# The latent attention's up-projections in three passes of split operands

## The reference

```python
def _mla(c_q, c_kv, k_r, z, cq_g, ckv_g, w_uq, w_ukv, q_g, k_g, cos, sin):
    bn, s, _ = c_q.shape
    q = (_rmsnorm(c_q, cq_g) @ w_uq).reshape(bn, s, MLA_HEADS, MLA_QK)
    kv = (_rmsnorm(c_kv, ckv_g) @ w_ukv).reshape(bn, s, MLA_HEADS, MLA_NOPE + MLA_V)
    k_nope, v = kv[..., :MLA_NOPE], kv[..., MLA_NOPE:]
    ...
    q = _rmsnorm(q, q_g)
    k = _rmsnorm(k, k_g)
```

## Time and profile before

| | |
|---|---|
| median of 3 runs | 1043.36 us (1043.26 to 1048.55) |
| span of the profiled execution | 1042.3 us |
| PE busy | 1016.2 us (97%) |
| DVE busy | 747.5 us (72%) |
| ACT busy | 571.0 us (55%) |
| DMA | 160.57 MB, mean 154 GB/s |
| chain that ended last | PE 86%, DVE 6%, ACT 3%, issue 3%, DMA 2% |

### The profile page before, as it was taken

How to read it: one execution, slowest core, us unless ns; L and a number is a source line. 1 busy time by engine, 2 the same in 40 slices (tenths; PEclk the granted TensorE clock), 3 DMA queues, 4 the chain that set the end, 5 groups by cost and what they waited for, 6 DMA issues and landing times.

```text
span 1042.3 us, 21750 instructions
## 1 busy us (share of the span) xinstructions
PE 1016.2 (97%) x9147; PEld 933.6 (90%) x9147; DVE 747.5 (72%) x1188; ACT 571.0 (55%) x841; POOL 71.9 (7%) x177
## 2 busy tenths in 40 slices
PE   9999999999999999999999999789999999999997
PEld 8878999999977999999998898769899899998885
DVE  5879677778777966778789868746778566555445
ACT  5775576444666658444468575125345466565333
POOL 8600000020000000001140000000000000000000
PEclk9999999999999999999999999999999999999999
DMA  9645453485664545348777350001355356555552
GB/s 320 187 135 164 141 152 113 153 259 167 190 184 134 150 136 160 115 145 243 171 194 215 109 166 24 24 22 43 122 168 180 123 160 182 177 186 183 193 189 81
DMA packets 73553, 160.57 MB, mean 154 GB/s; under 512 B 6917, under 2 KB 16320, under 8 KB 73456
## 3 DMA queue, kind: packets, MB, share of 16 engines
q1 hardware_dynamic: 70304, 150.59, 45.7%
q0 software_dynamic: 2832, 8.06, 4.0%
q10 hardware_dynamic: 320, 0.53, 0.1%
HBM read 158.11 MB, written 1.05 MB: 153 GB/s over the span
## 4 chain that ended last, share of the span: by engine, by line
PE 86%; DVE 6%; ACT 3%; issue 3%; DMA 2%; ACTq 0%; POOL 0%; DVEq 0%; POOLq 0%
PE psum L470 23%; PE psum L472 23%; PE psum L471 22%; PE psum L881 2%; PE psum L1033 1%; PE psum L870 1%; DVE ring_lo L1387 1%; DMA ring<-in_w_branch 1%; PE psum L722 1%; PE psum L700 1%; DVE arena L1573 1%; PE psum L1307 1%; PE psum L714 1%; PE psum L1324 1%; PE psum L704 1%
## 5 line engine op out<-in xcount | busy, mean ns | idle before, releaser
L1387 DVE TENSOR_TENSOR ring_lo<-ring,ring_hi 128x1024 fp32r<-128x1024 f32 (+4 forms) x291 | 342.4, 1194 | 175.2 <-ACT ring_hi L2446 173.3
L2446 ACT ACTIVATE ring_hi<-ring 128x1024 fp32r<-128x1024 f32 (+4 forms) x291 | 297.7, 1034 | 267.9 <-PE psum L472 241.9
L470 PE MATMUL psum<-hT,ring_hi 128*128 128x256 f32 x904 | 257.8, 285 | 2.5 <-issue 1.5
L472 PE MATMUL psum<-hT,ring_lo 128*128 128x256 f32 x904 | 255.0, 282 | 0.0
L471 PE MATMUL psum<-hT,ring_hi 128*128 128x256 f32 x904 | 254.7, 282 | 0.0
L470 PEld LDWEIGHTS psum<-hT,ring_hi 128*128 128x128 f32 x904 | 171.7, 190 | 5.1 <-issue 4.5
L472 PEld LDWEIGHTS psum<-hT,ring_lo 128*128 128x128 f32 x904 | 171.8, 190 | 0.0
L471 PEld LDWEIGHTS psum<-hT,ring_hi 128*128 128x128 f32 x904 | 171.7, 190 | 0.0
L470 PE MATMUL psum<-ring_hi,hT 128*128 128x512 f32 (+4 forms) x416 | 156.1, 375 | 2.1 <-DVE ring_lo L1387 1.5
L472 PE MATMUL psum<-ring_hi,hT 128*128 128x512 f32 (+4 forms) x416 | 151.9, 365 | 0.0
L471 PE MATMUL psum<-ring_lo,hT 128*128 128x512 f32 (+4 forms) x416 | 151.6, 364 | 0.0
(11 more groups left out here) (461 smaller groups left out, 1355.1 us busy)
## 6 DMA issues: line engine op xcount, KB each, us to landing
ring<-in_w_in SPq DMA_DIRECT2D x104, 512.0 KB, 3.4
ring<-in_w_ff SPq DMA_DIRECT2D x64, 512.0 KB, 3.5
ring<-in_w_branch SPq DMA_DIRECT2D x24, 512.0 KB, 3.5
ring<-in_w_out SPq DMA_DIRECT2D x24, 512.0 KB, 3.6
ring<-in_w_in SPq DMA_DIRECT2D x24, 384.0 KB, 3.3
ring<-in_w_xkv SPq DMA_DIRECT2D x16, 512.0 KB, 3.6
ring<-in_w_in SPq DMA_DIRECT2D x8, 528.0 KB, 3.6
ring<-in_w_xq SPq DMA_DIRECT2D x8, 512.0 KB, 3.8
```

What stands on the lines that cost most here:

```text
L470: mm(b, lhs[0], rhs[0], start=start, stop=False, **how)
L472: return mm(b, lhs[1], rhs[0], start=False, stop=stop, **how)
L1387: V.tensor_tensor(chunk_view(ring_lo, RAW, c), chunk_view(ring, RAW, c), plain(chunk_view(ring_hi, RING_HI, c)), ALU.subtract).then_inc(ev ...
L2446: AC(chunk_view(ring_hi, RING_HI, c), chunk_view(ring, RAW, c), ACT.Copy).then_inc(ev("whi_ready"), 1)
```

## The change

The up-projections use `split_mm`. For that the high halves of `wuq` and `wukv` are copied by ACT behind slot 1's copies, as soon as the layer's small weights have landed; DVE makes high and low halves of `cT` behind its copies, and the low halves of the two weights around the low half of chunk 15. PE waits for DVE's halves (`clo_ready`, `ulo_ready`) in place of the copies of `cT` and the landed weights. The low halves of the weights take the place of the weights themselves, the high ones lie in the arena where the gates come later.

```diff
+        cT_hi, cT_lo = at(arena_r, 3584, 3, S), at(arena_r, 4352, 3, S)
+        wuq_hi, wuq_lo = at(arena_r, 1024, 2, MH * MQK), at(arena_r, PB + 2048, 2, MH * MQK)
+        wukv_hi, wukv_lo = at(arena_r, 2560, 1024), at(arena_r, PB + 3584, 1024)
...
-                copied(pe, ("cT", l, 0), ("cT", l, 1))
-                pe.wait_ge(ev("layer_in"), 16 * N_LAYER_DMA * (l + 1))
+                pe.wait_ge(ev("clo_ready"), l + 1)
+                pe.wait_ge(ev("ulo_ready"), 2 * (l + 1))
                 for t in range(T):
+                    rows_t = slice(t * P, (t + 1) * P)
                     for h in range(2):
                         b = open_bank(pe, ("uq", l, t, h))
                         for k in range(2):
-                            m = mm(b[:, 0:384], cT[:, k, t * P:(t + 1) * P], wuq[:, k, h * 384:(h + 1) * 384],
-                                   start=(k == 0), stop=(k == 1))
+                            m = split_mm(b[:, 0:384], (cT_hi[:, k, rows_t], cT_lo[:, k, rows_t]),
+                                         [w[:, k, h * 384:(h + 1) * 384] for w in (wuq_hi, wuq_lo)], start=(k == 0), stop=(k == 1))
                         filled(m, ("uq", l, t, h))
                         b = open_bank(pe, ("ukv", l, t, h))
-                        filled(mm(b, cT[:, 2, t * P:(t + 1) * P], wukv[:, h * BANK:(h + 1) * BANK], start=True, stop=True),
+                        filled(split_mm(b, (cT_hi[:, 2, rows_t], cT_lo[:, 2, rows_t]),
+                                        [w[:, h * BANK:(h + 1) * BANK] for w in (wukv_hi, wukv_lo)], start=True, stop=True),
                                ("ukv", l, t, h))
...
+                copied(dve, ("cT", l, 0), ("cT", l, 1))
+                v(V.tensor_copy(cT_hi, cT))
+                vf(V.tensor_tensor(cT_lo, cT, plain(cT_hi), ALU.subtract), "clo_ready")
                 for t in range(T):
                     vf(V.tensor_copy(qk[:, t, MH:2 * MH, NOPE:MQK], bc(proj[:, t, COL_KR:COL_KR + ROPE], 1, MH)),
                       "kr_ready" if t else "dve")
 
-                weights_lo(2)
+                weights_lo(1)
+                dve.wait_ge(ev("uhi_ready"), 2 * l + 1)
+                vf(V.tensor_tensor(wuq_lo, wuq, plain(wuq_hi), ALU.subtract), "ulo_ready")
+                weights_lo(1)
+                dve.wait_ge(ev("uhi_ready"), 2 * l + 2)
+                vf(V.tensor_tensor(wukv_lo, wukv, plain(wukv_hi), ALU.subtract), "ulo_ready")
...
                 weights_hi(1)
                 p1(1)
+                act.wait_ge(ev("layer_in"), 16 * N_LAYER_DMA * (l + 1))
+                af(AC(wuq_hi, wuq, ACT.Copy), "uhi_ready")
+                af(AC(wukv_hi, wukv, ACT.Copy), "uhi_ready")
                 weights_hi(4)
```

## The result

| | before | after |
|---|---|---|
| median, same session | 1046.28 us (6 runs, 1043.26 to 1050.63) | 1052.28 us (6 runs, 1050.76 to 1054.69) |
| ratio, 95% interval | | 1.0057 [1.0035, 1.0079] |
| span of the profiled execution | 1042.3 us | 1052.6 us |

The change costs 6 us, where the prediction had 1.7, and 1052.28 lies above its range of 1042.5 to 1048.0. It missed by 7.2 us in absolute terms, and 2.9 of these lie in the base: 1043.36 was a median of three runs. Over 26 to 33 runs in each of four later sessions, each on another chip, the same kernel stands at 1045.65 to 1045.95, its single runs between 1041.3 and 1050.5. That leaves 4.3 us that the steps of the prediction don't hold.

What follows compares the result with a forecast made beforehand. PE was taken to bound the kernel, 97% busy. Its 3.2 us saving was to be lost waiting at slot 4, with delays added: 1043.36 + 1.39 + 0.30 = 1045.1 us, range 1042.5 to 1048.0.

Steps and rivals of the forecast that it cites:

- PE's saving: Up-projections of both layers: 7.0 us against 8.6, so PE saves 1.6 us per layer, 3.2 in all.
- DVE's and ACT's new work: In front of the gelu: added steps, with a 0.56 us copy, make its product 2.95 and 3.63 us late.
- The stall in front of slot 4: PE stands 2.9 and 1.9 us for banks 2 and 3; slot 4 starts 1.39 and 0.30 us later.
- Rival (b), the clock: Behind slot 4's stall PE returns at half pace, losing 2.0 us: once 1047.1 (chance 0.06), both layers 1049.1 (0.03).
- a sign that it is wrong: Behind the stalls at slot 4: a halved pace of PE would show the forecast wrong; it expected the same pace.
- The sum: Whole kernel: median 1043.36 plus delays of 1.39 and 0.30 us at slot 4 gives 1045.1 us.
- Behind that nothing gives them back: After slot 4's start: the chain through the query and key norms moves with PE, so the 1.7 us added stay.
- The base: Starting time of the kernel before, to which the delays were added: the median of the runs, 1043.36 us.
- Rival (a), the full saving: At slot 4 ACT's queue does not hold PE and all 3.2 us arrive: 1040.2 us, chance 0.06.

Runs made afterwards that it cites:

- ACT's and DVE's half alone: Changed kernel with plain products on PE, keeping ACT's and DVE's new work and PE's waits for it; 1047.47 us, ratio 1.0015 to the kernel before.
- ACT's order: Changed kernel with ACT's high halves of ring chunks 18 and 19 moved behind the first block's copies; 1052.65 us, ratio 1.0072 to the kernel before.
- the cold and the warm stall: Changed kernel with ten dummy products behind the second warming (cold), 1048.84 us; with six and four dummy products in front of slot 4 (warm), 1048.88 us.
- dummies early and late: Kernel before with twelve 16-column dummy products behind the second warming, 1048.84 us, or at 816 us behind the dense part, 1046.87 us.

## Why the prediction was wrong

- **PE's saving: right.** 7.0 us a layer, as worked out from the distances of starts; alone it shortens the two stretches by 1.53 and 1.54, where 1.6 stood.
- **DVE's and ACT's new work: right.** The copy 0.56 us (0.56), the gelu's tanh 3.01 and 3.69 late (2.95 and 3.63).
- **The stall in front of slot 4: right.** 2.72 and 1.73 us in the profile; counted as the prediction did, from the start of the last pass plus 0.23, they are 2.89 and 1.90 (2.9 and 1.9). They end with ACT's last copy of the first key-value block, the one that the sum used. Net growth 1.3 and 0.4 in the kernels without a fall of the clock (1.39 and 0.30). ACT's and DVE's half alone took 1.8 us more than before.
- **Rival (b), the clock: half right.** The pace behind the stall was halved in layer 0, which the prediction had named as a sign that it is wrong. The clock fell at the 2.7 and the 2.4 us stall of two traces and not at one of 2.6, nor at the two waits of 2.3 in ACT's order; at the 1.7 us stall of layer 1 in none. Its price in a trace is 1.7 us (2.0 was forecast). In the median no price can be told: the cold and the warm stall give the same time. One reason is in the traces: two to five half-clocked stretches of 3.4 us, each worth 1.7, stand between 530 and 800 us in every one of them, the kernel before's included (at 640, 667 and 691 us), and where they fall differs from trace to trace.
- **The sum: wrong, at its last step.** "Behind that nothing gives them back" took for granted that what lies behind the change moves as a block. The term that is missing is the price of 24 more records in front of the dense part: 2.6 to 3.5 us. The prediction wrote down the 24 records per layer that go and the 36 passes that come, costed their running time, and put their number at nothing. What the traces show in its place: the same code falls otherwise into blocks of 256 instructions, and PE pauses 7.0 us at their ends, where it paused 3.8. The row of the page that counts PE's records held the 24 in both kernels.
- **The base: 2.5 to 2.9 us low.** The forecast started from a median of three runs, while single runs of this kernel lie up to 8 us apart in one session; the later sessions put it 2.5 higher, the result's own 2.9. That is chance, no fault of the mechanism, but the range of 5.5 us left no room for it. The prediction gave 0.07 to a time over 1048.6, which is what came.

Put together by ratios: stalls 1.7 us and place 2.6 to 3.5 make 4.3 to 5.2 of the 6.0 that were measured (interval 3.7 to 8.3). The rest of 0.8 to 1.7 us may be the clock or chance; the runs don't tell.

Rival (a), the full saving, would have been wrong too, and for a reason that nobody named: even without any stall, the kernel stood at 1046.04 instead of 1042.8 (1045.9 less 3.1).

What is shown and what is argued: that the pauses and the time depend on the place in PE's stream is shown, with dummies early and late, and in both directions on the changed kernel. That the pauses that differ stand at every so many times 256 instructions is shown by the traces. That they are the fetching of instructions is argued from that. For it: the profile shows no engine, semaphore or transfer that PE waits for in them, and they come only where PE uses 256 instructions up in 5.7 us or less, among the shortest products (64 x 64). The Trainium skill, Runtime: NRT & Kernel Launch, section Instruction fetch mechanics, has each engine's instructions refilled in blocks of 256 by a DMA queue of its own, at a cost that is "mostly hidden". The traces agree with the blocks, and with "hidden" wherever a block takes longer than 5.7 us; in the dense part it isn't hidden, 2.5 to 7.5 us per execution in a kernel where PE is the bound. Why one place costs more than another is open: how long a pause is does not follow from the block's time alone, and the sum of pauses in one trace is no price of the time.

## What to carry to other kernels

Where the bound engine runs long stretches of very short instructions, an edit that changes its instruction count anywhere in front of them can cost or give some 3 us (0.3% here); try the same edit with the count restored, by a warming in fewer and wider products or a few tiny ones in a pause, before believing its time. Numbering the engine's instructions in the trace tells whether its unexplained pauses stand a fixed count apart. A gain that is exact in its own stretch and absent in the total has been lost elsewhere: compare the starts of the same instruction in both traces down to the end, and look at what is put down to issue. And work that is added in front of an in-order queue is paid at the far end of it: here four steps on DVE stalled PE through ACT's tanh, and moving two of them in front, with the rotary tables out of their way, took the whole stall away, where reordering ACT only moved it.

## What the hardware showed beyond that

- At the start of the program, 48 records of 64 columns took 10.50 us, 0.22 each, where the earlier trace rows have 24 of 128 columns in 5.00, 0.21 each: at these widths and at this pace the time of a warming goes by its products and not by their columns. It didn't warm either: the 14 records of 128 columns behind it took 3.19 us, 0.23 each, where the earlier trace rows have them in 1.73.

```profile
1.08 10.50 PE L651 MATMUL psum<-ones 128*128 128x64 f32 x48 [1.08 <-POOL ones L2988]
```

- A pass over operands in the reduced type takes 0.23 us at 512 columns from start to start, whether its operands come from the ring or were made by DVE a few microseconds before; at 384 columns it takes 0.175, over those as over `hT`.
